# Turning the recurrence's blocks as four 128x128 transposes, gating by channel, and one masked product replaced by a transpose

## The chip, the cores and the metric

One core of one Trainium2 chip runs the whole program once; nothing is shared with other cores. The metric is the time of that one execution on the device in microseconds (us). The engines are named as in the profile: PE is TensorE (matrix products and transposes, into PSUM), PEld its loading of the stationary operand, DVE is VectorE, ACT is ScalarE, POOL is GpSimd, SP is SyncE. Each engine works through its own list of instructions in order and waits on semaphores.

## What is computed

Two transformer layers of another kind follow this one; the change lies in the first, a hybrid layer on 512 tokens of width 1024. One of its two branches is an RWKV-7 recurrence with 8 heads of 64 channels, run forwards and backwards:

```python
def wkv7_scan(r, w, k, v, a, b, reverse):
    def step(S, inp):
        r_t, w_t, k_t, v_t, a_t, b_t = inp
        sa = jnp.einsum('bhij,bhj->bhi', S, a_t)
        S = S * w_t[:, :, None, :] + sa[..., None] * b_t[:, :, None, :] + v_t[..., None] * k_t[:, :, None, :]
        return S, jnp.einsum('bhij,bhj->bhi', S, r_t)
...
    g = jax.nn.sigmoid(xg) @ g_up
...
    y = ((wkv - mean) * lax.rsqrt(var + GN_EPS)).reshape(B, T, RWKV_DIM) * gn_w + gn_b
    y = y + bonus.reshape(B, T, RWKV_DIM).astype(jnp.float32)
    return (y * g).astype(u.dtype)
```

## The kernel before

**Tiles.** The recurrence is worked in 8 chunks of 64 tokens. A tile of it is 128x512: its upper 64 partitions are one head of a pair, its lower 64 the other, and its 512 columns are the 8 chunks of 64. It is stored either by channel (partition = channel, column = token of the chunk) or by token (partition = token within the chunk, column = channel). `turned` (L1020) goes from one to the other: 16 products of 64x64 with the 64x64 identity `ist`, one for each chunk and head, all in place. `each` (L1013) makes the 16 products of 64x64 of two tiles in the same way. On the chip such a product is two matmul instructions, so a group of 16 shows as x32 in the profile.

**Four pairs, two directions.** `recurrence_order` (L724) is the one list from which all engines take their order. For each head pair `pr` (0 to 3) there are preparation steps i = 5 to 28, and in each step direction d = 0 comes first and d = 1 second. Steps 5, 6, 7 turn Aa, Bb and Kt into An, Bn and Kn (`TURNS`). Steps 8 to 12 make the masked products of `MASKS`: MakT, Mrb, Mrk, Dm and Dt, where DVE multiplies the bank by the mask, and for Dt writes a second tile Lt with another mask. Step 13 is R0 = Dt + identity on DVE. Steps 14 to 28 are `PRODS`, which solve a triangular system by repeated squaring: Dt2, D2, R0a, D4 and so on; step 25 is KV, 26 Hc, 27 U1 and 28 W1T. ACT copies out the banks of An, Bn, Kn and the names in `BY_ACT`; DVE those of the others. For pair 0 steps 5 to 7 lie in `front_order`, among the products of the first projection.

**One bank for each direction.** `CHAIN_BANKS = ((4, 4), (5, 5))`: direction 0 has PSUM bank 4, direction 1 bank 5. So `clear(b)` makes PE wait, before each step of a direction, until the step before it has been copied out of the bank.

**What lies between.** After most steps `more()` gives PE one filler, six 128x512 or twelve 128x256 matmuls of the attention and gate projections, into banks 0 to 3. There is none after steps 5, 9, 14, 19 and 24, and after step 12 and step 13 (which has no product) there are two in a row. Beside the preparation of a pair DVE also normalises the pair before it (`rw_norming`, steps 5 to 13), normalises the next pair's keys (`rw_kk`), makes `halfL` = `ring` - `halfH` for each weight tile (ACT makes `halfH` first), and adds up one slice of another product in each step (`m_acc`, from `m_in`, which POOL loads by DMA). `rw_kk` and the transposes of the attention's q and k (the event "turn") share bank 6, with one waiting for the other's copy.

**Gate and turn.** In step 25 of pairs 1 to 3 `rw_gated` makes the gate by token (16 matmuls with `gup`, bank 4), and DVE multiplies y of the pair before by it; in step 27 `rw_turned` turns y by 16 products into bank 5, ACT copies it out as `yH` and DVE makes `yL` = bank - `yH`. The last pair's y is gated and turned in steps 11 to 14 of the attention that follows (`BETWEEN`, L793). `rw_values` turns v into `Vn` once for each pair, through bank 7.

Of the kernel before, what the change touches and what calls it, by code (L numbers as in the profile page):

```python
# [8 lines left out]
F32 = mybir.dt.float32  # L9
# [223 lines left out]
def program(nc, T, out):  # L233
# [175 lines left out]
    for d in range(2):  # L409
# [9 lines left out]
    PRODS = [("Dt2", "Dm", "Dt", None, "Dt"), ("D2", "Dt", "Dm", None, "Dt"), ("R0a", "D2", "R0", "R0", "D2"),  # L419
# [7 lines left out]
    MASKS = [("MakT", "Kt", "Aa", ("US", "LS")), ("Mrb", "Bb", "R", ("UI", "LI")), ("Mrk", "Kt", "R", ("UI", "LI")),  # L427
             ("Dm", "Aa", "Bb", ("DL", "DU")), ("Dt", "Bb", "Aa", ("DU", "DL"))]
# [295 lines left out]
    def recurrence_order():  # L724
# [25 lines left out]
        for pr in range(4):  # L750
# [3 lines left out]
            for i in range(i0, N_PREP):  # L754
                for d in range(2):
                    yield "prep", pr, d, i
                if (i - 4) * 19 // 24 > (i - 5) * 19 // 24:
                    yield from more()
                if pr < 3 and i < i0 + 5:
                    yield "kk", pr + 1, ("squares", "sums", "root", "inverse", "spread")[i - i0]  # L760
                if pr and 5 <= i < 14:
                    yield "norming", pr - 1, i - 5
                if pr and i in (25, 27):
                    yield ("gated", "turned")[(i - 25) // 2], pr - 1
                for _ in range(2 if not pr and i in (16, 20, 24) else 1):
                    yield "ada",
                yield from event(i > 8)
# [20 lines left out]
            for x in early:  # L788
# [4 lines left out]
    BETWEEN = {**{1 + i: ("norming", 3, i) for i in range(9)}, 11: ("gated", 3), 12: ("gated_out", 3), 13: ("turned", 3),  # L793
               14: ("turned_out", 3)}
# [74 lines left out]
    def tensor_program(pe):  # L869
# [189 lines left out]
        def rw_values(pr):  # L1059
            b = ADA_BANK  # L1060
            clear(b)
            pe.wait_ge(*at("us", 8 + pr))
            turned(bank(b), US[:, 8 + pr, :]).then_inc(*up("rw_pe", "v_turned", pr))
            free[b] = [("Vn", pr)]

        def rw_prep(pr, d, i):
            b = CHAIN_BANKS[d][i % 2]
            if 5 <= i < 8:
# [3 lines left out]
                turned(bank(b), piece(d, src)).then_inc(*up(f"rw_pe{d}", "pe", pr, d, name))  # L1072
                free[b] = [("ev", pr, d, name)]
            elif 8 <= i < 13:
# [82 lines left out]
        def rw_gated(pr):  # L1157
            b = CHAIN_BANKS[0][1]
            clear(b)
            for c in range(8):  # L1160
                for h in range(2):
                    i = pe.matmul(bank(b)[HP[h], c * 64:c * 64 + 64], US[:, 13, c * 64:c * 64 + 64],
                                  gup[:, (2 * pr + h) * 64:(2 * pr + h) * 64 + 64], start=True, stop=True)
            i.then_inc(*up("rw_pe", "gate", pr))
            free[b] = [("Y_gated", pr)]

        def rw_turned(pr):
            b = CHAIN_BANKS[1][1]
            clear(b)
            pe.wait_ge(*at("Y_gated", pr))  # L1170
            turned(bank(b), US[:, pr, :]).then_inc(*up("rw_pe", "y_turned", pr))
            free[b] = [("yL", pr)]
# [463 lines left out]
    def scalar_program(ac):  # L1636
# [104 lines left out]

        def rw_values(pr):
            ac.wait_ge(*at("v_turned", pr))
            if pr > 1:
                ac.wait_ge(*at("t3", pr - 2))
            if pr == 0:
                ac.wait_ge(*at("lsplit", FIRST_WOVEN - 1))
            ac.activation(Vn[pr % 2], bank(ADA_BANK), COPY).then_inc(*up("rw_act", "Vn", pr))
# [11 lines left out]
        def rw_prep(pr, d, i):  # L1760
            if 5 <= i < 8:
# [3 lines left out]
                ac.activation(piece(d, name), bank(CHAIN_BANKS[d][i % 2]),  # L1765
                              COPY).then_inc(*up(f"rw_act{d}", "ev", pr, d, name))
# [288 lines left out]
        def tables():  # L2055
# [3 lines left out]
                    "turned": rw_turned, "gemm": rw_gemm, "spill": rw_spill, "ms": a1_ms, "turn": a1_turn,  # L2059
# [34 lines left out]
        def a1_finish(hp):  # L2094
# [30 lines left out]
    def vector_program(ve):  # L2125
# [898 lines left out]
        def tables():  # L3024
            ve.wait_ge(*at("masks"))
            rope_tables("t1")
            for n, g in enumerate([col("gqk", 0)] + [col(f"gab{L}", g) for L in range(2) for g in (0, 2)]):
# [3 lines left out]
                    "loop": rw_loop, "norming": rw_norming, "gated": rw_gated, "turned": rw_turned, "ada": rw_ada, "mods_out": rw_mods_out,  # L3031
# [53 lines left out]
        def a1_finish(hp):  # L3085
# [338 lines left out]
```

## Time and profile before

| | |
|---|---|
| three runs | 2806.80, 2803.65, 2805.99 us (median 2805.99) |
| the profiled execution | 2804.09 us, of which its span is 2802.3 us |
| PE busy | 2696.4 us, 96% of the span |
| DVE busy | 1570.2 us, 56% |
| ACT busy | 926.3 us, 33% |
| the chain that ended last | PE 81%, DMA 8%, DVE 7%, ACT 3% |
| the recurrence (with its front) | about 92 to 610 us |

The chain is followed back from the last instruction, at each step to what released it. A row of the time line is: start in us, duration in us, engine, line, operation, out<-in, shapes, count, and in brackets the idle time before it with what ended it. Lines of one kind are merged, so a row of x64 is two groups of 16 products. A duration is that of the merged row from first start to last end, and since matmuls and ACT instructions overlap their neighbours, the distance from one start to the next start is what a piece costs its engine. A line number of the profile is that of the recording helper (L154 a matmul, L157 a transpose, L160 an ACT instruction, L163 a tensor_tensor), so the names of the tiles tell what it is; `slot` stands for any of the recurrence's scratch tiles.

### The profile page before, as it was taken

Reading aid. Unit: us, or ns where it says so; the run is one execution under the profiler, and the core shown is the slowest. Engines: PE = TensorE matmul, PEld = TensorE weight load, DVE = VectorE, ACT = ScalarE, POOL = GpSimd, SP = SyncE. Lnnn points to the kernel's source line nnn. Section 1 sums busy time; section 2 is a strip of 40 time slices with the busy share of each in tenths; the row PEclk is TensorE's granted clock in tenths of the full one; section 3 lists DMA queues with packets and bytes.
Section 4 is the critical chain, followed back from the end, with each engine's and each line's share of the span. In section 5 each row is a group of like instructions: output and inputs, shape, how many; then the busy total and the mean of one; then the engine's idle time right before and its main releaser. Section 6 shows DMA issues by size and latency. Waiting matters only on the chain.

```text
span 2802.3 us, 46790 instructions
## 1 busy us (share of the span) xinstructions
PE 2696.4 (96%) x20072; PEld 1996.9 (71%) x20072; DVE 1570.2 (56%) x2947; ACT 926.3 (33%) x1559; POOL 138.3 (5%) x237
## 2 busy tenths in 40 slices
PE   8999999999899999989999999999999999999999
PEld 6878777877643333357777778888877777788887
DVE  5767575766443333355685556665466864633443
ACT  6233333236301000033445542223334455332231
POOL 1010100010000000000000000000000000000000
PEclk9999999999999999999999999999999999999999
DMA  4233333264599999963352336664232532232332
GB/s 159 83 111 118 93 103 119 88 216 157 228 389 427 426 425 426 427 236 92 94 115 104 122 109 186 201 192 133 78 106 79 128 113 98 78 103 98 98 97 76
DMA packets 149990, 471.74 MB, mean 168 GB/s; under 512 B 14640, under 2 KB 41888, under 8 KB 137232
## 3 DMA queue, kind: packets, MB, share of 16 engines
q1 hardware_dynamic: 114720, 367.62, 36.6%
q0 software_dynamic: 24976, 82.71, 9.4%
q10 hardware_dynamic: 10080, 18.35, 2.2%
q8 instruction: 160, 2.62, 0.4%
q14 instruction: 54, 0.44, 0.1%
HBM read 451.05 MB, written 21.51 MB: 169 GB/s over the span
## 4 chain that ended last, share of the span: by engine, by line
PE 81%; DMA 8%; DVE 7%; ACT 3%; issue 1%; SPq 0%; ACTq 0%; POOL 0%; DVEq 0%
PE psum L154 78%; DMA wslot<-in_w_up 3%; DMA wslot<-in_w_gate 3%; PE psum L157 3%; DVE halfL L163 1%; DMA m_in<-in_w_ada 1%; DVE slot L163 1%; DVE X L163 1%; ACT halfH L160 1%; DVE vb L163 0%; DVE n_ht L169 0%; DVE gx L163 0%; DVE hL L169 0%; DVE m_acc L169 0%; DMA X<-in_x 0%
## 5 line engine op out<-in xcount | busy, mean ns | idle before, releaser
L163 DVE TENSOR_TENSOR halfL<-ring,halfH 128x1024 fp32r<-128x1024 f32 x302 | 367.9, 1220 | 531.3 <-ACT halfH L160 530.7
L160 ACT ACTIVATE halfH<-ring 128x1024 fp32r<-128x1024 f32 x302 | 317.2, 1053 | 691.7 <-PE psum L154 689.7
L154 PE MATMUL psum<-hH,halfH 128*128 128x512 f32 x1200 | 482.1, 402 | 1.7 <-DVE hL L169 1.7
L154 PE MATMUL psum<-hH,halfL 128*128 128x512 f32 x1200 | 469.1, 391 | 0.0
L154 PE MATMUL psum<-hL,halfH 128*128 128x512 f32 x1200 | 469.0, 391 | 0.0
L154 PEld LDWEIGHTS psum<-hH,halfH 128*128 128x128 f32 x1200 | 225.7, 188 | 74.8 <-issue 24.2
L154 PEld LDWEIGHTS psum<-hH,halfL 128*128 128x128 f32 x1200 | 225.8, 188 | 48.2
L154 PEld LDWEIGHTS psum<-hL,halfH 128*128 128x128 f32 x1200 | 226.0, 188 | 43.3
L154 PE MATMUL psum<-wslot,XT 128*64 128x512 f32 x1024 | 236.3, 604 | 20.0 <-DMA wslot<-in_w_gate 12.8
L154 PE MATMUL psum<-halfH,hH 128*128 128x512 f32 (+2 forms) x576 | 216.7, 376 | 3.7 <-DVE ks L163 1.8
L154 PE MATMUL psum<-halfL,hH 128*128 128x512 f32 (+2 forms) x576 | 207.2, 360 | 0.0
L154 PE MATMUL psum<-halfH,hL 128*128 128x512 f32 (+2 forms) x576 | 207.2, 360 | 0.0
L154 PEld LDWEIGHTS psum<-wslot,XT 128*64 128x64 f32 x1024 | 72.9, 138 | 158.7 <-issue 145.8
L163 DVE TENSOR_TENSOR X<-X,psum 128x512 f32<-128x512 f32 x136 | 88.2, 682 | 120.7 <-PE psum L154 120.7
L154 PEld LDWEIGHTS psum<-slot,slot 64*64 64x64 f32 x4096 | 124.3, 135 | 23.3 <-issue 12.8
L154 PE MATMUL psum<-slot,slot 64*64 64x64 f32 x4096 | 132.4, 219 | 6.2 <-DVE slot L163 2.3
L154 PE MATMUL psum<-halfH,aH 128*128 128x512 f32 x352 | 136.9, 389 | 0.0
L154 PE MATMUL psum<-halfL,aH 128*128 128x512 f32 x352 | 136.9, 389 | 0.0
L154 PE MATMUL psum<-halfH,aL 128*128 128x512 f32 x352 | 136.9, 389 | 0.0
L154 PEld LDWEIGHTS psum<-halfH,hH 128*128 128x128 f32 x576 | 108.6, 188 | 30.4 <-issue 8.6
L169 DVE SCALAR_TENSOR_TENSOR m_acc<-m_in,cact,m_acc 128x512 f32<-128x512 f32 (+1 forms) x126 | 116.3, 923 | 20.6 <-DMA m_in<-in_w_ada 20.0
L154 PEld LDWEIGHTS psum<-halfH,hL 128*128 128x128 f32 x576 | 108.7, 189 | 17.0
(492 smaller groups left out, 4106.3 us busy)
## 6 DMA issues: line engine op xcount, KB each, us to landing
wslot<-in_w_gate SPq DMA_DIRECT2D x32, 2048.0 KB, 25.0
wslot<-in_w_down SPq DMA_DIRECT2D x32, 2048.0 KB, 25.9
ring<-in_w_in SPq DMA_DIRECT2D x120, 512.0 KB, 3.7
wslot<-in_w_up SPq DMA_DIRECT2D x30, 2048.0 KB, 25.9
ring<-in_w_gu SPq DMA_DIRECT2D x88, 512.0 KB, 3.6
m_in<-in_w_ada POOLq DMA_DIRECT2D x96, 256.0 KB, 3.1
m_in<-in_w_ada POOLq DMA_DIRECT2D x48, 512.0 KB, 4.9
ring<-in_w_down SPq DMA_DIRECT2D x44, 512.0 KB, 3.6
```

Source lines behind the costliest of these rows:

```text
L154: return self.e.matmul(*a, **k)
L157: return self.e.transpose(*a, **k)
L160: return self.e.activation(*a, **k)
L163: return self.e.tensor_tensor(*a, **k)
L169: return self.e.scalar_tensor_tensor(*a, **k)
```

## The change

- **Turns.** `turned_by_two` takes the place of `turned` for An, Bn, Kn, v and y: four 128x128 transposes, each over both heads and two chunks. In the result the block of head h and chunk 2n+c stands at partitions of c and columns of h, so it isn't where the tile wants it. `sorted_out` copies the bank out on ACT in four instructions, each 64 partitions by 4x64 columns, two of them crossing from one half of the partitions to the other.
- **Dm.** `MASKS` begins with Dt (step 8); MakT, Mrb and Mrk follow in steps 9 to 11; in step 12 Dm is the turn of the masked Dt, by `turned_by_two` and `sorted_out` on ACT. DVE's mask for Dm is gone, and the first two of `PRODS` wait for Dm.
- **Gate.** y is turned first (step 25, bank 5), while still ungated, and copied by ACT into `US`; then the gate is one product of `gup` and `US` by channel (step 27, bank 4), DVE multiplies, ACT makes `yH` from `US`, and DVE makes `yL` in a step of its own ("low", step 28). In `BETWEEN` the last pair's steps are turned 11, turned_out 12, gated 13, gated_out 14, low 15.
- QT keeps the old `turned`.

```diff
-    PRODS = [("Dt2", "Dm", "Dt", None, "Dt"), ("D2", "Dt", "Dm", None, "Dt"), ("R0a", "D2", "R0", "R0", "D2"),
+    PRODS = [("Dt2", "Dm", "Dt", None, "Dm"), ("D2", "Dt", "Dm", None, "Dm"), ("R0a", "D2", "R0", "R0", "D2"),
...
-    MASKS = [("MakT", "Kt", "Aa", ("US", "LS")), ("Mrb", "Bb", "R", ("UI", "LI")), ("Mrk", "Kt", "R", ("UI", "LI")),
-             ("Dm", "Aa", "Bb", ("DL", "DU")), ("Dt", "Bb", "Aa", ("DU", "DL"))]
+    MASKS = [("Dt", "Bb", "Aa", ("DU", "DL")), ("MakT", "Kt", "Aa", ("US", "LS")), ("Mrb", "Bb", "R", ("UI", "LI")),
+             ("Mrk", "Kt", "R", ("UI", "LI"))]
...
-                if pr and i in (25, 27):
-                    yield ("gated", "turned")[(i - 25) // 2], pr - 1
+                if pr and i in (25, 27, 28):
+                    yield {25: "turned", 27: "gated", 28: "low"}[i], pr - 1
...
+        def turned_by_two(o, x):
+            for n in range(0, 512, 128):
+                i = pe.transpose(o[:, n:n + 128], x[:, n:n + 128], ident)
+            return i
...
+            elif i == 12:
+                clear(b)
+                pe.wait_ge(*at("ev", pr, d, "Dt"))
+                turned_by_two(bank(b), piece(d, "Dt")).then_inc(*up(f"rw_pe{d}", "pe", pr, d, "Dm"))
+                free[b] = [("ev", pr, d, "Dm")]
...
-            for c in range(8):
-                for h in range(2):
-                    i = pe.matmul(bank(b)[HP[h], c * 64:c * 64 + 64], US[:, 13, c * 64:c * 64 + 64],
-                                  gup[:, (2 * pr + h) * 64:(2 * pr + h) * 64 + 64], start=True, stop=True)
-            i.then_inc(*up("rw_pe", "gate", pr))
+            pe.matmul(bank(b), gup[:, pr * 128:pr * 128 + 128], US[:, 13, :], start=True,
+                      stop=True).then_inc(*up("rw_pe", "gate", pr))
...
+        def sorted_out(o, b):
+
+            to, of = o.rearrange("p (n c x) -> p n c x", c=2, x=64), b.rearrange("p (n h x) -> p n h x", h=2, x=64)
+            for c in range(2):
+                for h in range(2):
+                    i = ac.activation(to[HP[h], :, c, :], of[HP[c], :, h, :], COPY)
+            return i
...
-            ve.tensor_tensor(yL[pr], bank(CHAIN_BANKS[1][1]), yH[pr].bitcast(F32), SU).then_inc(*up(R_, "yL", pr))
+            ve.tensor_tensor(yL[pr], US[:, pr, :], yH[pr].bitcast(F32), SU).then_inc(*up(R_, "yL", pr))
```

PE in steps 5 to 7 of pair 1, first as it was (slot_145, _146, _147 are Aa, Bb, Kt of direction 0; _155, _156, _157 those of direction 1), then as it is:

```order
L154 MATMUL psum<-con,slot_145 64x64 x16
L154 MATMUL psum<-con,slot_155 64x64 x16
L154 MATMUL psum<-con,slot_146 64x64 x16
L154 MATMUL psum<-con,slot_156 64x64 x16
...
L154 MATMUL psum<-con,slot_144 128x2 x4
L154 MATMUL psum<-con,slot_147 64x64 x16
L154 MATMUL psum<-con,slot_157 64x64 x16
```

```order
L157 MATMUL psum<-con,slot_145 128x128 x4
L157 MATMUL psum<-con,slot_155 128x128 x4
L157 MATMUL psum<-con,slot_146 128x128 x4
L157 MATMUL psum<-con,slot_156 128x128 x4
...
L154 MATMUL psum<-con,slot_144 128x2 x4
L157 MATMUL psum<-con,slot_147 128x128 x4
L157 MATMUL psum<-con,slot_157 128x128 x4
```

Nothing moves here; each group of 16 becomes one of 4, with the fillers where they were.

DVE in steps 7 to 9 of pair 1, before and after. slot_140/_150 are MakT of the two directions, slot_142/_152 Dt, slot_143/_153 Lt, kk_n and slot_160 belong to the next pair's keys, US to the normalisation of the pair before:

```order
L163 TENSOR_TENSOR halfL_81<-ring_76,halfH_78 128x1024 [waits split_act]
L163 TENSOR_TENSOR US<-US,mean 128x512 [waits rw_dve]
L169 SCALAR_TENSOR_TENSOR m_acc_136<-m_in_134,cact,m_acc_136 128x512 [waits side_dve,m_in0]
L163 TENSOR_TENSOR slot_140<-psum,con 128x512 [waits rw_pe0]
L163 TENSOR_TENSOR slot_150<-psum,con 128x512 [waits rw_pe1]
L166 TENSOR_SCALAR kk_n<-kk_n 128x8 [waits rw_act]
L184 RECIPROCAL kk_n<-kk_n 128x8 [waits rw_dve]
L163 TENSOR_TENSOR US<-US 128x512 [waits rw_dve]
L169 SCALAR_TENSOR_TENSOR m_acc_136<-m_in_135,cact,m_acc_136 128x512 [waits side_dve,m_in1]
L163 TENSOR_TENSOR Mrb_114<-psum,con 128x512 [waits rw_pe0]
```

```order
L163 TENSOR_TENSOR halfL_81<-ring_76,halfH_78 128x1024 [waits split_act]
L163 TENSOR_TENSOR US<-US,mean 128x512 [waits rw_dve]
L169 SCALAR_TENSOR_TENSOR m_acc_136<-m_in_134,cact,m_acc_136 128x512 [waits side_dve,m_in0]
L163 TENSOR_TENSOR slot_142<-psum,con 128x512 [waits rw_pe0]
L163 TENSOR_TENSOR slot_143<-psum,con 128x512
L163 TENSOR_TENSOR slot_152<-psum,con 128x512 [waits rw_pe1]
L163 TENSOR_TENSOR slot_153<-psum,con 128x512
L166 TENSOR_SCALAR kk_n<-kk_n 128x8 [waits rw_act]
L184 RECIPROCAL kk_n<-kk_n 128x8 [waits rw_dve]
L163 TENSOR_TENSOR US<-US 128x512 [waits rw_dve]
L169 SCALAR_TENSOR_TENSOR m_acc_136<-m_in_135,cact,m_acc_136 128x512 [waits side_dve,m_in1]
L163 TENSOR_TENSOR slot_140<-psum,con 128x512 [waits rw_pe0]
```

The four masks of Dt and Lt stand in step 8 instead of two of MakT, and every mask after them one step later.

PE in steps 25 to 28 of pair 1, before and after. slot_141,slot_146 and slot_151,slot_156 are Hc, slot_141,slot_148 and slot_151,slot_158 are W1T; left out are the fillers and U1:

```order
L154 MATMUL psum<-gup,US 64x64 [waits rw_act0]
...
L154 MATMUL psum<-slot_141,slot_146 64x64 [waits rw_dve]
...
L154 MATMUL psum<-slot_151,slot_156 64x64 [waits rw_act1]
...
L154 MATMUL psum<-con,US 64x64 [waits rw_act1]
...
L154 MATMUL psum<-slot_141,slot_148 64x64 [waits rw_act0]
...
L154 MATMUL psum<-slot_151,slot_158 64x64 [waits rw_dve]
```

```order
L157 MATMUL psum<-con,US 128x128 [waits rw_dve,rw_act1]
...
L154 MATMUL psum<-slot_141,slot_146 64x64 [waits rw_act0]
...
L154 MATMUL psum<-slot_151,slot_156 64x64 [waits rw_act]
...
L154 MATMUL psum<-US,gup 128x512 [waits rw_act0]
...
L154 MATMUL psum<-slot_141,slot_148 64x64 [waits rw_dve]
...
L154 MATMUL psum<-slot_151,slot_158 64x64 [waits rw_act1]
```

In step 26 it is now direction 1 that waits, for ACT's copy of the turned y; in step 28 direction 0 waits for DVE's gating, and direction 1 no longer waits for `yL`.

## Rows read from the trace of the kernel before

**Rows 1.** Stretches: us; busy (x count) of PE, PEld, DVE, ACT, POOL; PEclk; DMA.
```profile
272.00:408.00 136.00, 132.06 (x2285) 109.03 (x2280) 89.54 (x182) 42.80 (x68) 12.91 (x24) 1.00 0.34 103
...
620.00:660.00 40.00, 34.50 (x461) 26.03 (x462) 24.52 (x91) 28.99 (x81) 1.63 (x2) 1.00 0.44 163
```

**Rows 2.** Waits of PE, 84 to 620 us: total, times, longest.
```profile
PE psum L154 <- DVE slot L163: 3.3, 6, 1.4
PE psum L154 <- ACT slot L160: 2.4, 6, 0.5
```

**Rows 3.** Time line of PE, pair 2, steps 5 to 7.
```profile
378.25 3.95 PE L154 MATMUL psum<-con,slot 64*64 64x64 f32 x128
382.13 0.50 PE L154 MATMUL psum<-halfH,hH 128*128 128x512 f32 x1
...
383.63 2.96 PE L154 MATMUL psum<-con,slot 128*128 128x2 f32 x72
```

**Rows 4.** Time line of PE: four transposes, a 512-column product (x2), v's turn.
```profile
195.02 0.60 PE L157 MATMUL psum<-con,Zst 128*128 128x128 f32 x4
195.55 1.09 PE L154 MATMUL psum<-colb,slot 64*64 64x1 f32 x32
...
332.57 1.12 PE L154 MATMUL psum<-US,lora 64*128 64x512 f32 x2
...
342.54 1.15 PE L154 MATMUL psum<-con,US 64*64 64x64 f32 x32
343.47 0.33 PE L154 MATMUL psum<-st,W1T 64*64 64x64 f32 x4
```

**Rows 5.** Time line and groups of ACT: copies of 512 and 256 columns, 64 partitions.
```profile
195.65 0.69 ACT L160 ACTIVATE stage<-psum,g 128x512 f32<-128x512 f32 x1 [0.47 <-PE psum L157]
...
288.47 0.38 ACT L160 ACTIVATE Zst<-psum 128x256 f32<-128x256 f32 x1
288.75 0.38 ACT L160 ACTIVATE psum<-psum 128x256 f32<-128x256 f32 x1
...
379.44 0.60 ACT L160 ACTIVATE slot<-psum 128x512 f32<-128x512 f32 x1 [9.33 <-PE psum L154]
...
L160 ACT ACTIVATE US<-US 64x512 f32<-64x512 f32 x1 | 0.6, 633 | 1.2 <-DVE US L169 1.2
```

**Rows 6.** Time line of ACT, DVE and PE, pair 1, steps 7 to 10.
```profile
253.13 1.05 ACT L160 ACTIVATE halfH<-ring 128x1024 fp32r<-128x1024 f32 x1
...
254.21 1.23 DVE L163 TENSOR_TENSOR halfL<-ring,halfH 128x1024 fp32r<-128x1024 f32 x1 [6.29 <-ACT halfH L160]
...
256.62 1.28 DVE L163 TENSOR_TENSOR slot<-psum,con 128x512 f32<-128x512 f32 x2
...
261.60 0.66 PE L157 MATMUL psum<-con,Zst 128*128 128x128 f32 x4 [0.79 <-DVE slot L163]
```

**Rows 7.** Time line of PE: products 14 to 15 begin, pairs 2 and 3.
```profile
408.81 3.36 PE L154 MATMUL psum<-slot,slot 64*64 64x64 f32 x108
...
544.56 3.95 PE L154 MATMUL psum<-slot,slot 64*64 64x64 f32 x128
```

**Rows 8.** Time line of PE, pair 1, steps 25 to 28.
```profile
313.95 1.15 PE L154 MATMUL psum<-gup,US 128*64 128x64 f32 x32
315.90 2.08 PE L154 MATMUL psum<-slot,slot 64*64 64x64 f32 x64 [0.79 <-DVE US L163]
...
323.10 1.15 PE L154 MATMUL psum<-con,US 64*64 64x64 f32 x32
...
325.67 1.15 PE L154 MATMUL psum<-slot,slot 64*64 64x64 f32 x32 [0.49 <-DVE yL L163]
326.75 0.50 PE L154 MATMUL psum<-hH,halfH 128*128 128x512 f32 x1
```

**Rows 9.** Time line of ACT and PE in the front, after step 7 of pair 0.
```profile
110.46 2.06 ACT L160 ACTIVATE U<-psum 128x512 f32<-128x512 f32 x4
...
111.20 0.47 PE L154 MATMUL psum<-halfH,hH 128*128 128x512 f32 x1 [1.28 <-ACT U L160]
```

More of the change, by code:

```diff
@@ L790, in recurrence_order @@
         assert not events and not sums
-    BETWEEN = {**{1 + i: ("norming", 3, i) for i in range(9)}, 11: ("gated", 3), 12: ("gated_out", 3), 13: ("turned", 3),
-               14: ("turned_out", 3)}
+    BETWEEN = {**{1 + i: ("norming", 3, i) for i in range(9)}, 11: ("turned", 3), 12: ("turned_out", 3), 13: ("gated", 3),
+               14: ("gated_out", 3), 15: ("low", 3)}
     def chunk_at(d, s):
@@ L1062, in rw_values @@
             pe.wait_ge(*at("us", 8 + pr))
-            turned(bank(b), US[:, 8 + pr, :]).then_inc(*up("rw_pe", "v_turned", pr))
+            turned_by_two(bank(b), US[:, 8 + pr, :]).then_inc(*up("rw_pe", "v_turned", pr))
             free[b] = [("Vn", pr)]
@@ L1071, in rw_prep @@
                 pe.wait_ge(*at("ev", pr, d, "Aa"))
-                turned(bank(b), piece(d, src)).then_inc(*up(f"rw_pe{d}", "pe", pr, d, name))
+                turned_by_two(bank(b), piece(d, src)).then_inc(*up(f"rw_pe{d}", "pe", pr, d, name))
                 free[b] = [("ev", pr, d, name)]
-            elif 8 <= i < 13:
+            elif i == 12:
[3 more added lines that the diff above has]
+                free[b] = [("ev", pr, d, "Dm")]
+            elif 8 <= i < 12:
                 name, left, right, _ = MASKS[i - 8]
@@ L1169, in rw_turned @@
             clear(b)
-            pe.wait_ge(*at("Y_gated", pr))
-            turned(bank(b), US[:, pr, :]).then_inc(*up("rw_pe", "y_turned", pr))
-            free[b] = [("yL", pr)]
+            pe.wait_ge(*at("Y_sum", pr))
+            turned_by_two(bank(b), US[:, pr, :]).then_inc(*up("rw_pe", "y_turned", pr))
+            free[b] = [("yT", pr)]
         def modulation(L):
@@ L1747, in rw_values @@
                 ac.wait_ge(*at("lsplit", FIRST_WOVEN - 1))
-            ac.activation(Vn[pr % 2], bank(ADA_BANK), COPY).then_inc(*up("rw_act", "Vn", pr))
+            sorted_out(Vn[pr % 2], bank(ADA_BANK)).then_inc(*up("rw_act", "Vn", pr))
         def rw_early(pr, d, x):
@@ L1764, in rw_prep @@
                 ac.wait_ge(*at("pe", pr, d, name))
-                ac.activation(piece(d, name), bank(CHAIN_BANKS[d][i % 2]),
-                              COPY).then_inc(*up(f"rw_act{d}", "ev", pr, d, name))
+                sorted_out(piece(d, name), bank(CHAIN_BANKS[d][i % 2])).then_inc(*up(f"rw_act{d}", "ev", pr, d, name))
+            elif i == 12:
+                ac.wait_ge(*at("pe", pr, d, "Dm"))
+                sorted_out(piece(d, "Dm"), bank(CHAIN_BANKS[d][i % 2])).then_inc(*up(f"rw_act{d}", "ev", pr, d, "Dm"))
             elif i >= 14 and PRODS[i - 14][0] in BY_ACT:
@@ L1779, in rw_turned, with rw_gated @@
             ac.wait_ge(*at("y_turned", pr))
-            ac.activation(yH[pr], bank(CHAIN_BANKS[1][1]), COPY).then_inc(*up("rw_act", "yH", pr))
+            sorted_out(US[:, 4 + pr, :], bank(CHAIN_BANKS[1][1])).then_inc(*up("rw_act", "yT", pr))
+        def rw_gated(pr):
+            ac.wait_ge(*at("Y_gated", pr))
+            ac.activation(yH[pr], US[:, pr, :], COPY).then_inc(*up("rw_act", "yH", pr))
         spilled, turned_last = [0], [None]
```

20 lines of the change are left out of this document (10 added, 10 removed).

## The prediction

> **What bounds the kernel now.** The page first: PE is busy for 96% of the span and 81% of the chain that ended last lies on it. The change lies between 92 and 610 us, so I read the stretches next: from 272 to 408 us PE is busy for 132.06 of 136 us at full clock, DVE for two thirds, ACT for one third [rows 1]. In this stretch every microsecond that PE doesn't need is a microsecond won, unless PE then waits for a copy out of its bank. The waits tell how near that is: from 84 to 620 us PE stood 3.3 us for DVE's tiles and 2.4 us for ACT's [rows 2]. Little is waited now because the fillers just cover the copies. So the question is not what the transposes save, but where the cover ends. For that I walked the time lines of PE, ACT and DVE through each pair.
>
> **Prices.** Four old turns run from 378.25 to 382.13 us: 0.97 us each [rows 3]. Four 128x128 transposes of the same form take 195.02 to 195.55, 0.53 us [rows 4]. So a turn gives PE 0.44 us back. The copy on ACT was 0.60 us. It becomes four pieces of 256 columns; two copies of that size start 0.28 us apart and one lasts 0.38 [rows 5], and 64 partitions by 512 columns take 0.63 us, as much as 128 by 512 [rows 5], so I price by columns: 3 x 0.28 + 0.38 = 1.22 us until the tile is there, 4 x 0.28 = 1.12 us of ACT. No row shows the piece itself; from below it can't be cheaper than those 0.28, from above it costs at most what full copies cost, 2.06 us for four, (2.06 - 0.60) / 3 = 0.49 apart [rows 9]. I take 0.28, since the column count is what the rows of ACT differ by. ACT starts 0.63 us after the first transpose (195.02 to 195.65 [rows 4, 5]); from the end of a copy to PE I take 0.05 us, an estimate from there being no gap in the four groups of [rows 3], whose third needs the copy that ends at 380.04 [rows 5].
> The Trainium skill ("ScalarE: Activation LUTs", What ACT_TABLE_LOAD costs) gives an ACTIVATE without pointers 186 ns + 0.833 ns an element with 93 ns overlap: by it a piece is 0.40 us, 0.31 us apart, and the four take 1.32 us instead of 1.22, which would take 1 to 2 us off my sum.
>
> **Gross.** 24 turns of An, Bn, Kn, 4 of v, 4 of y and 8 of Dm: 40 x 0.44 = 17.6 us. The gate gives nothing: its 16 matmuls last 1.15 us as the profile has them [rows 8], and the nearest single product of 512 columns, the one with `lora`, 1.12 us [rows 4].
>
> **What of it is lost, step by step.**
> *Steps 5 and 6* have no filler between them. From PE's first transpose: copy d0 0.63 to 1.85, PE takes step 6 d0 at 1.90; copy d1 can only start at 1.75 (ACT), ends at 2.97; step 6 d1 at 3.02, filler at 3.55. Before: 3.88 [rows 3]. So four turns give 0.33 us, not 1.76: over four pairs 1.3.
> *Step 7* has fillers on both sides (1.50 us [rows 3]) and keeps its 0.9 a pair. The Bn copies end before it is due, the Kn copies before step 8 is.
> *Pair 0* does this in the front, and there the copies of U stand behind those of Kn on ACT and PE already waits 1.28 us for the first [rows 9]. Two Kn copies of 1.12 in place of 0.5 push U back: PE resumes 0.35 us later than now, so its 1.2 is gone. v gives 0.5, step 10 waits 0.3 for MakT's mask, step 12 gives 0.9: together 0.75.
> *Steps 8 to 11.* Dt and Lt in step 8 put 4 masks of 0.64 (2.5 us) where 2 stood (1.28 [rows 6]), just before step 9, after which there is no filler. In **pair 1** DVE comes late to them whatever PE does: ACT makes `halfH` only behind Kn (253.13, unchanged, since Kn's copy is longer), then halfL at 254.21, then two more, so the masks begin at 256.62 [rows 6], when PE is already 1.2 us ahead. Direction 0 of step 9 waits until 257.9, the keys' product and MakT's masks follow, and the transposes that now stand at 261.60 [rows 6] come at 262.55, 0.95 late. Step 12 gives 0.9 back: at product 14 pair 1 has won nothing. In **pair 2** the `halfH` comes before Kn and DVE is free: the same walk puts product 14 at 406.7 instead of 408.81 [rows 7], 2.1 won. In **pair 3** DVE idles before step 8; the waits left are 0.3 (step 10) and 0.9 (step 11, where it waits 1.1 already), and product 14 comes at 542.6 instead of 544.56 [rows 7], 1.95 won.
> *Step 12* has two fillers behind it and no product in 13, 4 us for two copies that need 0.63 + 2 x 1.12: hidden. If that cover were gone it would cost 1 us a pair.
> *DVE* loses 8 masks, 5 us, none of it on the path by itself.
> *Steps 25 and 26:* now gate to filler is 1.0 + 0.79 of wait + 2.0 = 3.95 us (the next filler after 315.90 is 2.0 later) [rows 8]. Then: turn 0.53, Hc d0 1.0, d1 waits for y's copy until 0.63 + 1.22 + 0.05 = 1.90, ends 2.9: 1.05 won in pairs 1 and 3, 0.85 in pair 2. *Steps 27 and 28:* now 323.10 to 326.75, 3.65 [rows 8]; then the gate 1.05, W1T d0 waits for DVE's product (0.2 + 0.69 + 0.05), then 2.0: 4.0, so 0.35 lost each. Three pairs: 2.95 - 1.05 = 1.9.
> *v in the loops:* 0.93 (342.54 to 343.47) to 0.53 [rows 4], 3 x 0.4 = 1.2; its copy has idle ACT around it.
> *The last pair's y* lies in the attention, where ACT is the busy engine (29 of 40 us [rows 1]): the turn is shorter, but ACT gets 1.2 us more. I put nothing, with 1 us either way.
> What follows (merges, experts) is started by these steps' ends and moves along.
>
> **Sum.** 0.75 + 0 + 2.1 + 1.95 in the preparations, 1.9 for y, 1.2 for v: 7.9, say 8 us of 17.6. Against the profiled execution 2804.09 - 8 = 2796.1; that execution lies 1.9 us under the median of the runs, so 2798.
>
> **Rivals.**
> 1. *The covers hold better.* DVE has 5 us less to do and part of the 3.3 us that PE waits for it [rows 2] goes as well; pair 1 recovers. Gain 12 to 18, time 2788 to 2794. For it: DVE is a third idle. Against: an in-order list fixes when it comes to the masks.
> 2. *The Dt masks cost every pair what they cost pair 1.* Then pairs 2 and 3 lose their 2 us each as well: gain 4, time 2802, within 0.2%. For it: it is enough that `halfH` or an `m_acc` (waiting for its DMA) comes 1 to 2 us later; against: the walks of both pairs had DVE idle ahead of step 8.
> 3. *Slower: the piece is priced by instruction, not by column.* At 0.49 us apart a copy takes 2.07 us. Steps 5 and 6 then take 5.2 us instead of 3.88 (1.7 worse than forecast, four times), steps 7 and 8 wait for the Bn and Kn copies (2 us a pair), Dm's copies outlast their fillers (0.4), y's copy holds Hc (0.85 three times): 19 us, against the 8 won, 2806 + 11 = 2817. It decides from 0.28 + 0.21 x 8 / 19 = 0.37 us a piece. Against it: 0.28 for 256 columns [rows 5].
> 4. *The clock.* In 620 to 660 us a group of four transposes stands every 2 us and the granted clock is 1.00 [rows 1], the 2.4 GHz level. Were it to fall to 1.2 GHz for the 10 us around steps 5 to 8 of each pair, 40 us would be lost: 2838. The Trainium skill ("TensorE: Matmul & The Clock Gate", Part 4: PE-mode transpose) says that transposes don't count as activity for the clock; this trace shows no fall where they are mixed with products.
>
> **Chances.** My walk 0.50 (2794 to 2800), rival 1 0.10, rival 2 and kin 0.30, rival 3 0.08, the clock 0.02. A measurement of this kernel can tell about 0.2% (5.6 us) from no change: faster by more 0.60, within 0.30, slower 0.10. Range: up to the edge of rival 1's half, 2789, and over rival 2 with some waits more, 2808; rivals 3 and 4 are left out.
>
> **What would show it.** Steps 5 and 6 of pair 2 at 3.5 us from first transpose to filler (3.88 now), with PE waiting for ACT's tiles: in all about 10 us of such waits where 2.4 are. ACT's pieces at 0.38 us, 0.28 apart. In pair 1 PE waits for DVE before step 9, about 1.5 us, and product 14 starts no earlier against step 5 than now (31.1 us); in pairs 2 and 3 about 2 us earlier. Step 25 to filler 2.9 us, step 27 to filler 4.0. PE's busy time down by 15 to 18 us. Wrong would be the whole if ACT's piece were over 0.37 us apart or the clock showed under 1.00 in these stretches; wrong in size if DVE were late in pair 2 or 3, or early in pair 1.

## The result, and the profile after

The changed kernel takes 2818.39 us, median of five runs (2811.32 to 2823.75), against 2805.99 before: ratio 1.0045, 95% interval 1.0033 to 1.0057, slower by 12.6 us. Forecast were 2798 us and a range up to 2808. The profiled execution took 2819.83 us with a span of 2818.0, and the granted clock over the whole was 0.988 where it had been 0.994.

PE's busy time fell by only 8 us (2696.4 to 2688.5), and PE waits more. First its waits from 84 to 670 us in the trace after (total, times, longest), against [rows 2], whose two sums are the same when the trace before is read to 670 us:

```profile
PE psum L157 <- ACT slot L160: 9.0, 8, 1.8
PE psum L154 <- DVE slot L163: 6.7, 7, 2.3
PE psum L154 <- ACT slot L160: 5.6, 10, 1.6
PE psum L154 <- ACT U L160: 4.2, 1, 4.2
```

The first row is the transposes themselves (L157), waiting for ACT to empty the bank. It had no counterpart before. Some stretches of the trace after, with the columns of [rows 1]; the last but two is the granted clock, which was 1.00 in all of them before:

```profile
112.00:142.00 30.00, 27.66 (x335) 23.05 (x336) 20.09 (x32) 8.39 (x16) 1.61 (x3) 0.89 0.27 80
...
240.00:272.00 32.00, 26.73 (x320) 21.55 (x320) 17.50 (x34) 13.92 (x31) 2.15 (x4) 0.89 0.26 75
...
378.00:408.00 30.00, 27.59 (x327) 21.88 (x323) 17.78 (x40) 12.64 (x28) 1.75 (x4) 0.94 0.24 74
```

**Where the time goes** can be read by laying the same step of PE side by side in both time lines. The lag (start after minus start before):

| step of PE | before | after | lag |
|---|---|---|---|
| pair 0, step 5 | 98.25 | 98.47 | 0.2 |
| pair 0, first masked product (step 8) | 123.58 | 127.85 | 4.3 |
| pair 0, product 14 | 143.58 | 146.94 | 3.4 |
| pair 1, step 5 | 244.25 | 247.88 | 3.6 |
| pair 1, step 8 | 254.11 | 258.36 | 4.3 |
| pair 1, product 14 | 275.36 | 283.22 | 7.9 |
| pair 1, product 19 | 292.00 | 304.43 | 12.4 |
| pair 2, step 5 | 378.25 | 391.50 | 13.3 |
| pair 2, product 14 | 408.81 | 421.79 | 13.0 |
| pair 3, step 5 | 514.57 | 528.61 | 14.0 |
| pair 3, product 14 | 544.56 | 558.33 | 13.8 |
| attention, first scores | 614.17 | 628.17 | 14.0 |

So the front and pair 1 lose nearly all of it, 12.4 us. Pairs 2 and 3 break even up to product 14, and what follows product 19 in pair 1 and product 14 in pair 2 loses about 1 us each. At the large product stages the lag is 12.6 (the run that starts at 1663.57 us before, 1676.18 after). By the end of the span it is 15.7: the profiled execution after loses 3 us more behind 2030 us, in work that the change doesn't touch. Its granted clock there is 0.82 in 2032 to 2040 us and 0.79 in 2112 to 2120 and 2448 to 2456 us, where the trace before has 1.00 in the same work. That part I don't count to the change; the medians differ by 12.4 us.

*The front.* Time line of PE after, from step 5 of pair 0:

```profile
98.47 1.03 PE L157 MATMUL psum<-con,slot 128*128 128x128 f32 x8
101.28 0.66 PE L157 MATMUL psum<-con,slot 128*128 128x128 f32 x4 [1.77 <-ACT slot L160]
102.85 0.66 PE L157 MATMUL psum<-con,slot 128*128 128x128 f32 x4 [0.91 <-ACT slot L160]
...
108.81 1.03 PE L157 MATMUL psum<-con,slot 128*128 128x128 f32 x8
114.04 0.77 PE L154 MATMUL psum<-halfH,hH 128*128 128x512 f32 x1 [4.19 <-ACT U L160]
114.60 0.63 PE L154 MATMUL psum<-halfL,hH 128*128 128x512 f32 x1
```

Two turns take 1.03 us, as forecast, and then PE stands 1.77, 0.91 and, after step 7, 4.19 us; the last was 1.28 in [rows 9]. The products behind it last 0.63 us and start 0.43 apart, where 0.39 and 0.23 is normal: ten of them, 2.1 us more, until the clock is back at 118.8 us.

*Pair 2, steps 5 to 7*, the place of [rows 3]: PE first, then ACT.

```profile
391.50 1.03 PE L157 MATMUL psum<-con,slot 128*128 128x128 f32 x8
393.73 0.66 PE L157 MATMUL psum<-con,slot 128*128 128x128 f32 x4 [1.20 <-ACT slot L160]
395.30 1.11 PE L157 MATMUL psum<-con,slot 128*128 128x128 f32 x4 [0.91 <-ACT slot L160]
396.06 0.78 PE L154 MATMUL psum<-halfH,hH 128*128 128x512 f32 x1
396.64 0.63 PE L154 MATMUL psum<-halfL,hH 128*128 128x512 f32 x1
```
```profile
392.13 3.12 ACT L160 ACTIVATE slot<-psum 64x256 f32<-64x256 f32 x8 [8.68 <-PE psum L157]
395.27 3.12 ACT L160 ACTIVATE Bn<-psum 64x256 f32<-64x256 f32 x8
398.41 1.06 ACT L160 ACTIVATE halfH<-ring 128x1024 fp32r<-128x1024 f32 x1
```

Eight pieces in 3.12 us: 0.39 us apart, each 378 ns long, so they don't overlap. A copy takes 1.57 us; the forecast was 1.22. From the first transpose to the filler it is 4.56 us (3.88 before, 3.55 forecast), and the filler itself runs slow.

*Pair 1* shows what stands behind the pieces on ACT's list. ACT, DVE and PE after, steps 7 to 9, the place of [rows 6]:

```profile
256.63 3.12 ACT L160 ACTIVATE Kn<-psum 64x256 f32<-64x256 f32 x8 [1.86 <-PE psum L157]
259.77 1.06 ACT L160 ACTIVATE halfH<-ring 128x1024 fp32r<-128x1024 f32 x1
```
```profile
260.86 1.23 DVE L163 TENSOR_TENSOR halfL<-ring,halfH 128x1024 fp32r<-128x1024 f32 x1 [9.21 <-ACT halfH L160]
...
263.27 2.48 DVE L163 TENSOR_TENSOR slot<-psum,con 128x512 f32<-128x512 f32 x4
```
```profile
264.61 3.17 PE L154 MATMUL psum<-slot,slot 64*64 64x64 f32 x64 [2.06 <-DVE slot L163]
267.70 1.69 PE L154 MATMUL psum<-con,kk_n 128*64 128x128 f32 x16
```

`halfH` comes 6.64 us later than before (253.13): 3.6 of it is the lag with which pair 1 begins, 1.3 the later start of Kn's pieces behind step 5, and 1.7 their length. DVE waits 9.21 us for it with the masks queued behind, PE waits 2.06 us for the masks, and then works at the lower clock: 3.17 us for what takes 2.08. The same chain comes a second time, behind Dm's copies:

```profile
281.62 3.12 ACT L160 ACTIVATE slot<-psum 64x256 f32<-64x256 f32 x8 [0.40 <-ACT stage L160]
284.76 1.06 ACT L160 ACTIVATE halfH<-ring 128x1024 fp32r<-128x1024 f32 x1
```
```profile
285.85 1.23 DVE L163 TENSOR_TENSOR halfL<-ring,halfH 128x1024 fp32r<-128x1024 f32 x1 [6.93 <-ACT halfH L160]
...
295.75 0.75 DVE L169 SCALAR_TENSOR_TENSOR m_acc<-m_in,cact,m_acc 128x512 f32<-128x512 f32 x1 [2.76 <-DMA m_in<-in_w_ada]
```
```profile
287.49 2.08 PE L154 MATMUL psum<-slot,slot 64*64 64x64 f32 x64 [1.55 <-ACT slot L160]
...
297.16 2.08 PE L154 MATMUL psum<-slot,slot 64*64 64x64 f32 x64 [2.33 <-DVE slot L163]
```

DVE is held from 278.9 to 285.85 us, so it gives the modulation's `m_in` buffers back late, their next loads land late, and the sum that PE wants for product 17 stands behind an `m_acc` that waits for its DMA. (This last link, from the buffers to the loads, is read from the order of the rows; no run tries it by itself.) That costs 4.6 us between product 14 and 19 (21.21 us against 16.64).

### The profile page after: what moved, and what is told of

Read it like the earlier page. It is cut to its first block, busy times and chain, and to the rows that moved or that the text cites. A ratio compares the mean times of both kernels' runs of the same rounds, so it can differ in the third digit from the quotient of the medians.

```text
span 2818.0 us, 44435 instructions
## 1 busy us (share of the span) xinstructions
PE 2688.5 (95%) x18832; PEld 1985.4 (70%) x18832; DVE 1565.6 (56%) x2939; ACT 970.4 (34%) x1691; POOL 137.6 (5%) x237
## 4 chain that ended last, share of the span: by engine, by line
PE 80%; DMA 8%; DVE 6%; ACT 4%; issue 2%; ACTq 0%; SPq 0%; POOL 0%; DVEq 0%
PE psum L154 76%; PE psum L157 4%; DMA wslot<-in_w_gate 3%; DMA wslot<-in_w_up 3%; DVE halfL L163 1%; ACT slot L160 1%; ACT halfH L160 1%; DVE X L163 1%; DMA m_in<-in_w_ada 1%; DVE slot L163 0%; DVE vb L163 0%; ACT Kn L160 0%; DVE gx L163 0%; DMA X<-in_x 0%; DVE b_ss L175 0%
## 5 line engine op out<-in xcount | busy, mean ns | idle before, releaser
L154 PEld LDWEIGHTS psum<-slot,slot 64*64 64x64 f32 x3840 | 117.9, 135 | 33.1 <-issue 12.3
L154 PE MATMUL psum<-slot,slot 64*64 64x64 f32 x3840 | 126.6, 221 | 14.1 <-DVE slot L163 6.2
```

Source lines behind the costliest of these rows:

```text
L154: return self.e.matmul(*a, **k)
```

## Experiments

Three theories stood after this reading. **A**: the copy in four pieces (1.57 us against 0.60) holds PE at steps 5 to 7 and everything behind it on ACT. **B**: Dt first, and Dm as a turn, cost it in pair 1. **C**: the granted clock falls around the transposes; whether through PE's idle time or through the transposes themselves was to be told apart. In the edits shown, `+` is the kernel of the run, and lines are shortened. Each kernel ran against the kernel before on the same chip; ratios are to that.

### One part undone: the turns of An, Bn and Kn (e1)

```
-   turned_by_two(bank(b), piece(d, src))       # PE, steps 5 to 7
+   turned(bank(b), piece(d, src))
-   sorted_out(piece(d, name), bank(...))       # ACT
+   ac.activation(piece(d, name), bank(...), COPY)
```

> The changed kernel, but An, Bn and Kn (steps 5 to 7) turned by 64x64 matmuls and copied in one piece as before; v, y, the gate, Dt first and Dm as a turn of Dt stay. Theory A (the copy in four pieces holds PE, and whatever stands behind it on ACT, in steps 5 to 7): the profile of the change puts 4.0 us of the lag in the front (PE waits 4.19 us for U) and some 2 us more in steps 5 to 7 of each later pair, so 8 to 12 of the 12.4 us come back: 2806 to 2810 us, and PE's 4.19 us wait for U falls back to 1.3. Theory B (Dt first, with its two masks a direction, and Dm's turn behind it cost it, 9 us in pair 1 between the first mask product and QT): the time stays at 2813 or above, and pair 1's waits of 2.06 us (first masks) and 2.33 us (product 17) stay.

2806.3 us, ratio 0.9997 (0.9989 to 1.0006). Between 1.0045 and this lie 13.5 us: undoing the 24 turns two by two takes the whole loss away, as A has it, with about 4 us of uncertainty either way. Its waits show U back at what it was:

```profile
PE psum L154 <- ACT U L160: 1.3, 1, 1.3
```

B isn't nothing, though: PE's waits of 1.55 us (product 15) and 1.86 us (product 17) of pair 1 stand in this trace too, and from product 14 to 19 it needs 20.3 us against 16.6. So the rest of the change wins about as much elsewhere as Dm's turn loses there.

### The copy shared between two engines (e2)

```
-   sorted_out(piece(d, name), bank(...))            # ACT: four pieces
+   sorted_out(piece(d, name), bank(...), (0,))      # ACT: two
+   for h in range(2):                               # DVE: the other two
+       ve.tensor_copy(to[HP[h], :, 1, :], of[HP[1], :, h, :])
```

> The changed kernel, but of the four 64x256 pieces of each copy of An, Bn and Kn two are on ACT and two on DVE, side by side; all else stays. Theory A: a copy takes 0.78 us in place of 1.56, shorter than the 0.97 us of an old turn, so steps 5 to 7 hold PE no longer and the gross gain is kept: 2796 to 2804 us, faster than before or equal. Theory B: 2810 or above, since the masks are as they were. Theory C (TensorE's granted clock falls because of the 128x128 transposes themselves, whatever they wait for): the granted clock in 92 to 142 us stays near 0.93 and the matmuls behind the turns still take 0.63 us in place of 0.39, some 5 us in all: 2803 to 2809.

2811.32 us, ratio 1.0013 (1.0004 to 1.0022): better than the change by 9 us, but not the 2796 to 2804 that I expected of A. The copy is shorter only where DVE is free. Its pieces take 427 ns, and in the front it was not free; its group, and PE there:

```profile
L181 DVE COPY slot<-psum 64x256 f32<-64x256 f32 x16 | 6.8, 427 | 1.4 <-PE psum L157 1.1
```
```profile
102.51 1.98 PE L157 MATMUL psum<-con,slot 128*128 128x128 f32 x8 [2.58 <-DVE slot L181]
104.15 0.77 PE L154 MATMUL psum<-hH,halfH 128*128 128x512 f32 x1
```

DVE did its part only behind `halfL`, which waited for ACT's `halfH`; PE stood 2.58 us and the clock fell, with the wait moved from ACT to DVE. In 92 to 142 us, where I had named a clock near 0.93 as the mark of the transposes as cause, it is 0.97: 0.72 in 102 to 108 us, around that wait, and 1.00 from 112 us on.

### The pieces alone, no transpose (e3, e12)

```
-   ac.activation(piece(d, name), bank(...), COPY)                    # kernel before
+   for h in HP:
+       for x in (0, 256):
+           ac.activation(piece(d, name)[h, x:x + 256], bank(...)[h, x:x + 256], COPY)
```

> The kernel before, but each copy of An, Bn and Kn by ACT is in four pieces of 64x256 (contiguous halves, the same result); no transpose, no other part of the change. Theory A: the pieces stand 0.39 us apart, a copy takes 1.56 us in place of 0.60, longer than the 0.97 us between two turns; 1.2 to 1.8 us in steps 5 and 6 of each pair, 2 us at U in the front, and what ACT does behind it (half H, masks on DVE) 1 to 2 us late in pair 1: 2812 to 2817 us. Theory B, or theory C with the transposes as the cause of the fall of the clock: at most 2809, granted clock 0.994 as before.

2813.06 us, ratio 1.0022 (1.0013 to 1.0031): the kernel before with nothing but its copies cut in four loses 6 us, half of what the change loses. It is the second proof of A, here without the rest. ACT, and PE in the front behind its wait for U:

```profile
99.64 2.64 ACT L160 ACTIVATE slot<-psum 64x256 f32<-64x256 f32 x8
```
```profile
113.73 0.47 PE L154 MATMUL psum<-halfH,hH 128*128 128x512 f32 x1 [2.57 <-ACT U L160]
...
115.20 0.63 PE L154 MATMUL psum<-halfH,hH 128*128 128x512 f32 x1
```

The lower clock (0.63 us a product) comes here too, 1.5 us after PE has resumed, and this kernel has no transpose there. But its pieces stand 0.33 us apart, not 0.39. They differ from the change's in two things: 256 columns in a row, and each on its own partitions. e12 has the first as in the change (every other chunk of 64) and the second as in e3:

> As e3 (the kernel before, copies of An, Bn and Kn in four pieces), but each piece takes every other chunk of 64 columns, read and written so, on its own partitions. e3's pieces stood 0.33 us apart and the change's 0.39. If the chunks of 64 make the difference: 0.39; if the move to other partitions does: 0.33.

```profile
100.09 2.64 ACT L160 ACTIVATE slot<-psum 64x256 f32<-64x256 f32 x8
```

Again 0.33. So the chunks cost nothing; what is left as the difference are the pieces that write to the other 64 partitions (and with it the order of the pieces over the partitions, which wasn't tried by itself). e12 took 2811.75 us in its one run.

### PSUM laid out for the reader (e8)

```
-   pe.transpose(o[:, n:n + 128], x[:, n:n + 128], ident)
+   pe.transpose(to[:, n], x[:, n * 128:n * 128 + 128], ident)   # to: "p (h n x) -> p n h x"
```

> The changed kernel, but the turns write PSUM so that each of the four pieces is read as 256 consecutive words of a partition, and only written in chunks of 64; same instructions, same order. The pieces stood 0.39 us apart in the change and 0.33 in e3, where both sides were consecutive and no piece changed its partitions. If the strided read is the difference: 0.33 apart, a copy takes 1.34 us in place of 1.57, and 1 to 3 us less than the change: 2815 to 2817. If the move to other partitions or the strided write is: 0.39 as before and 2817 to 2820.

2819.26 us, ratio 1.0049 (1.0036 to 1.0062), the change's time. Its pieces are as far apart:

```profile
99.63 3.11 ACT L160 ACTIVATE slot<-psum 64x256 f32<-64x256 f32 x8
```

With e12 this closes the layout as a cause.

### PE's waits filled with work (e4, e9)

```
+   if (i, d) == (6, 0):
+       unused(16)
+   if (i, d) == (6, 1):
+       unused(10)
...
+   for m in range(n):                       # unused(n)
+       pe.matmul(bank(ADA_BANK)[h, cc], SL[0]["Aa"][h, cc], ist[h, :], start=True, stop=True)
```

> The changed kernel with 64x64 matmuls that nobody reads put where PE waits in its trace: 16 ahead of step 6 of the first direction (gap 1.20 us), 10 ahead of the second (gap 0.91), 56 behind step 7 of pair 0 (gap 4.19), 30 ahead of step 9 of pair 1 (gap 2.06). The waits themselves stay as they are. If PE's idle time is what lets the granted clock fall behind the turns (slow rows of 0.63 us for 0.39, and 3.17 for 2.08: 2.2 us in the front, 1.4 and 1.7 in pair 1, 1.7 in pair 2, 7 us in all), the clock stays at 1.00 there and the time falls to 2810 to 2813. If the transposes are the cause, or the slow rows lie in time that waits hide, 2817 to 2821.

2810.91 us, ratio 1.0013 (1.0004 to 1.0021): 9 us under the change (4 either way), for matmuls that nobody reads. The front, with 56 of them (112 records) behind step 7:

```profile
106.86 1.03 PE L157 MATMUL psum<-con,slot 128*128 128x128 f32 x8
107.82 3.48 PE L154 MATMUL psum<-con,slot 64*64 64x64 f32 x112
112.08 0.47 PE L154 MATMUL psum<-halfH,hH 128*128 128x512 f32 x1 [0.78 <-ACT U L160]
```

U comes as late behind step 7 as in the change (5.2 us); the product behind it takes 0.47 us and not 0.77, and the granted clock is 1.00 in 112 to 120 us where the change has 0.58, and in 262 to 270 and 394 to 402 us, where it has 0.79 and 0.79. So C holds, with PE's idle time as the trigger at these places. Does it have to be products? e9 fills the same places with 128x128 transposes:

> As e4, but the stretches in which PE waits are filled with 128x128 transposes that nobody reads (7, 4, 26 and 14 of them, about the same time as the 64x64 matmuls of e4). If the granted clock falls because PE stands idle: the clock stays at 1.00 behind the turns as in e4, ratio 1.0005 to 1.0020. If PE's transposes don't hold the clock up: it falls as in the change (slow rows of 0.63 us behind the turns, 0.58 granted in 112 to 120 us), ratio 1.0035 to 1.0055.

2811.04 us, ratio 1.0026 (1.0015 to 1.0037), 5 us under the change (again 4 to 5 either way). The ratio lies between what I had named for the two theories; the records decide:

```profile
107.18 3.87 PE L157 MATMUL psum<-con,slot 128*128 128x128 f32 x34
112.41 0.47 PE L154 MATMUL psum<-halfH,hH 128*128 128x512 f32 x1 [1.36 <-ACT U L160]
```

34 transposes in a row, 1.36 us of wait, and the product behind runs at full speed; the clock is 1.00 in the same three stretches. Here transposes held it up as products did. The clock costs 5 to 9 us of the loss by these two kernels; by the slow rows of the change I had counted 7.

Not every wait has that effect. In the change, full speed follows on waits of 1.77 and 0.91 us in steps 5 and 6 of pair 0, on 1.20 and 0.92 us in pair 3, and on 2.33 us at product 17 of pair 1, while 1.20 and 0.91 us were enough in pairs 1 and 2. In e4 the clock falls at another place, 0.79 in 280 to 288 us, where nothing was filled. What tells these cases apart the runs don't show.

### The order of the masks, and Dm's turn (e5, e6)

e5 is the kernel before with Dt first, e6 the change with Dm by its own product and the old order.

```
-   MASKS = [("MakT", ...), ("Mrb", ...), ("Mrk", ...), ("Dm", ...), ("Dt", ...)]
+   MASKS = [("Dt", ...), ("MakT", ...), ("Mrb", ...), ("Mrk", ...), ("Dm", ...)]      # e5
```

> The kernel before, but Dt first among the five masked products (Dt, MakT, Mrb, Mrk, Dm), Dm still by its own product; no transpose in blocks of 128 is added. Theory B (the order alone costs it, since the first masks on DVE are four in place of two): PE's wait behind the first masks grows by 1.2 us and stays in pair 1, where e1 had nothing to spare: 2808 to 2811. Theory B2 (the order is nearly free; what costs in e1, 3.4 us between product 14 and product 19 of pair 1, is Dm's copy in pieces on ACT, which holds the stage copies and half H, and by half H the modulation's loads): at most 1 us, 2806 to 2808, and no wait above 1 us at products 15 and 17 of pair 1.

2806.37 us, ratio 1.0000 (0.9989 to 1.0011). The order alone costs nothing that can be measured. In its trace pair 1 needs 16.4 us from product 14 to 19, as before, and doesn't wait at products 15 and 17; so what e1 loses there (20.3 us) comes from Dm's turn and its copies, not from the order.

> The changed kernel, but Dm by its own masked product and the masks in the old order; An, Bn, Kn, v and y are turned two by two and sorted out as in the change. Theory A: steps 5 to 7 keep their cost, and of the masks' part 4.2 us of PE time is given up (four times 1.05) while some 5 to 7 us of pair 1's waits go: 2812 to 2817. Theory B (order and Dm's turn are the whole loss): 2803 to 2808.

2819.3 us, ratio 1.0039 (1.0025 to 1.0053). The median is a little above my span for A, the ratio (some 2816 us) inside it, and both are far from B. Of its waits, those for ACT in the turns and for U are the change's; that for DVE is 1.8 us shorter, and PE's other wait for ACT's tiles is 2.4 us as in the kernel before, where the change has 5.6:

```profile
PE psum L157 <- ACT slot L160: 9.0, 8, 1.8
PE psum L154 <- DVE slot L163: 4.9, 7, 1.7
PE psum L154 <- ACT slot L160: 2.4, 6, 0.5
PE psum L154 <- ACT U L160: 4.2, 1, 4.2
```

So Dm as a turn in all pairs is worth nothing that can be measured (1.0045 with it, 1.0039 without). That it saves in pairs 0, 2 and 3 what it gives away behind product 14 of pair 1 is how I read it; e10 below bears it out.

### The front alone (e11)

```
-   turned_by_two(bank(b), piece(d, src))
+   (turned_by_two if pr else turned)(bank(b), piece(d, src))    # and ACT's copy likewise
```

> The changed kernel, but An, Bn and Kn of pair 0 alone (in the front) turned and copied as before. The change's trace puts 4.0 us of the lag between step 5 and the first masks of pair 0 (PE waits 4.19 us for U in place of 1.28, and 11 matmuls behind it take 0.63 us in place of 0.39): the ratio falls by 0.0014 from the change's 1.0045, to 1.0025 to 1.0037. If pairs 1 to 3 give the time away whatever the front does, it stays above 1.004.

2809.83 us, ratio 1.0016 (1.0002 to 1.0031): 8 us back for six of the 24 turns, where I had read 4 off the trace; the interval is wide enough for both. Its own trace has 24.5 us from step 5 of pair 0 to the first masked product (98.17 to 122.68), where the change takes 29.4: 4.9 us back in the front itself. Another 3 come at 616 to 624 us, where the change's clock is 0.79 and that of e11 is 1.00. By the traces the front costs 4 to 5 us and pair 1 about 9.

### What is worth keeping (e7, e10)

> Only v, y and the gate of the change: An, Bn, Kn turned and copied as before, the masks as before. From the change's trace: y 0.67 us less a pair between product 25 and the bonus for pairs 0 to 2, v 0.5 less three times and once in the front, pair 3's y in the attention stage 0.7 more (2.3 us of wait for the sorted y, 1.6 for yL before): 3 us less than before, 2802 to 2805. If the covers are worse than those rows say, 2806 to 2808.

e7 (only v, y and the gate) took 2804.45 us, ratio 0.9997 (0.9988 to 1.0006): with the measurement's width, between nothing and the 3 us I had worked out. The loop of pair 2 gives some of it back: PE waits 2.4 us for `SA` there, 1.5 before; its cause I didn't follow.

e10 takes all that paid: v, y and the gate, and Dm as a turn except in pair 1.

```
+   elif i == 12 and pr == 1:
+       each(bank(b), piece(d, "Aa"), piece(d, "Bb"))     # Dm by its own product
    elif i == 12:
        turned_by_two(bank(b), piece(d, "Dt"))
```

> A version meant to be the best of the parts: v, y and the gate of the change, Dt first, Dm as a turn of Dt in pairs 0, 2 and 3 and by its own masked product in pair 1, An, Bn and Kn turned as before. Against e1, pair 1 gets back the 3.4 us between products 14 and 19: 2801 to 2804, ratio 0.9985 to 0.9992. If PE's time that Dm's turn saves is waited away in the other pairs too: as e7, 0.9992 to 1.0002.

2802.49 us, ratio 0.9989 (0.9979 to 0.9999), 3 us under the kernel before (0.3 to 6) and the fastest of all. Pair 1 has its 16.4 us from product 14 to 19 back:

```profile
273.40 3.95 PE L154 MATMUL psum<-slot,slot 64*64 64x64 f32 x128
...
289.83 2.39 PE L154 MATMUL psum<-slot,slot 64*64 64x64 f32 x72
```

## Why the prediction was wrong, step by step

- **What bounds the kernel** (PE, with covers that just hold [rows 1, 2]) was right, and so was the question where the cover ends. The PE price was right too: 0.53 us a turn, 1.03 for two.
- **The copy: this term failed.** I took 0.28 us between pieces from two copies of 128 partitions [rows 5], with 0.28 and 0.49 as bounds and 0.37 as the point from which the change loses. It measured 0.39. The row of 64 partitions by which I argued that columns set the price reads and writes `US`, so it isn't a copy out of a bank at all. The row that I chose as nearest was near in columns, but its copies stayed on their partitions; e3 and e12 have 0.33 for such pieces of 64 partitions, and 0.39 comes with the change's own, two of which cross over. Both lie above the value that I took. By the formula of the Trainium skill ("ScalarE: Activation LUTs", What ACT_TABLE_LOAD costs), which it gives for tiles of 128 partitions, a piece of 256 columns is estimated at 0.40 us. The 378 ns here come near to that, but where the page has 93 ns of overlap between neighbours, e3 shows 0.04 us and the change none.
- **Steps 5 and 6**: 3.55 forecast, 4.56 measured. With 1.57 us a copy the walk as I wrote it gives 4.35 (copy d1 ends at 0.63 + 3.14, then 0.05, and 0.53 for step 6 d1); the other 0.2 is the slow clock, which makes those last transposes take 0.76. The walk was right; its number was not.
- **Pair 0**: forecast +0.75, measured -3.1 (lag 0.2 to 3.4). I had U 0.35 us later; it was 2.84 us later (113.30, before 110.46). Of this 1.0 is that step 7 itself begins later, behind the waits of steps 5 and 6, and 1.7 that from Kn's first piece to U it is now 3.14 us in place of 1.43. ACT's `halfH` stands ahead of Kn's copies in both kernels and is not the cause. The clock's 2.1 us stands on top.
- **Pair 1**: I forecast nothing won, on the ground that ACT makes `halfH` at 253.13 whatever Kn's copy does. That sentence failed first: `halfH` stands behind Kn's copies on ACT, and these took 3.12 us, 1.4 times what I had priced and twice what they took before, and began later. The second loss, behind Dm's copies, was missing altogether. I wrote of step 12 "4 us for two copies that need 0.63 + 2 x 1.12: hidden", which looks at PE's need alone and not at `halfH` and the stage copies behind those copies on ACT. Of the 8.8 us that pair 1 loses from step 5 to product 19, 4.6 are this.
- **Pairs 2 and 3**: 2.1 and 1.95 forecast, 0.3 and 0.3 measured from step 5 to product 14 (30.56 to 30.29, 29.99 to 29.72). What Dm's turn gives there steps 5 and 6 take.
- **y and v**: turn to filler 2.9 us forecast, 3.31 measured; gate to filler 4.0 forecast, 4.1 measured (rows below, of pair 1). With v I had summed 3.1 us; e7 measures 0.8 with some 2.5 either way. (For the gate as it was I wrote 1.0 + 0.79 + 2.0, which is 3.79; the 3.95 that I used is right by [rows 8], where the gate lasts 1.15.) The last pair's y, which I put at nothing with 1 us either way, loses 1.6: the lag is 14.0 at the first scores and 15.6 at its first product (`yH`, 659.88 before, 675.44 after). By 1663 us all of that and more has come back.

```profile
326.29 0.60 PE L157 MATMUL psum<-con,US 128*128 128x128 f32 x4
...
328.52 1.15 PE L154 MATMUL psum<-slot,slot 64*64 64x64 f32 x32 [0.56 <-ACT US L160]
329.60 0.50 PE L154 MATMUL psum<-hH,halfH 128*128 128x512 f32 x1
...
334.69 1.02 PE L154 MATMUL psum<-US,gup 128*128 128x512 f32 x2
336.76 2.08 PE L154 MATMUL psum<-slot,slot 64*64 64x64 f32 x64 [1.06 <-DVE US L163]
338.78 0.50 PE L154 MATMUL psum<-hH,halfH 128*128 128x512 f32 x1
```

- **The rivals.** Rival 3 named the mechanism (the piece dearer than its columns) and gave 2817; I gave it 0.08. It assumed 0.49 apart; at 0.39 its own line gives 19 x 0.11 / 0.21 - 8 = 2 us lost. The other 10 it didn't have: the clock (5 to 9), and the chain over `halfH` and `m_in`. Rival 4, the clock, was right that it falls around steps 5 to 8, and wrong in size (7 us, not 40: PE works for 3 to 5 us at the lower level, not 10, and in pair 3 not at all) and in cause: it asked whether transposes hold the clock up, while here it fell behind waits of PE and stayed up when they were filled. My evidence against it, a clock of 1.00 in 620 to 660 us, came from a stretch whose longest wait of PE is 1.64 us; the change made one of 4.19. The Trainium skill's rule that I cited beside it ("TensorE: Matmul & The Clock Gate", Part 4: PE-mode transpose), that transposes don't count as activity for the clock, isn't borne out by e9, where the clock stayed at 1.00 through 34 fp32 transposes.
- **The chances** had the two rivals that came true together at 0.10, as if they were independent of the walk. They weren't: the longer copy makes the waits, and waits let the clock fall.

## What to carry to other kernels

When one instruction on a helper engine becomes four, price it by a row of the same shape and the same move between partitions, or take the upper bound: here 0.11 us a piece turned a forecast gain into a loss. And follow that engine's list past the consumer in question: what stands behind the longer copies (here a weight conversion, through it DVE, through DVE a load) may wait for longer than PE does. Where PE is the bound, a wait can cost more than its length, since the work behind it may run at a lower clock (2.1 us on top of 4.19 in the front).

## What the runs showed of the hardware that I had not expected

- ACT's copies from PSUM of 64 partitions by 256 columns: 0.33 us apart on their own partitions (372 ns each, read in a row or in every other chunk of 64), 0.39 apart in the change, where two of four go to the other partitions (378 ns each, no overlap). DVE's take 427 ns.
- In the front of the change the granted clock is 0.99 in 110 to 112 us and 0.50 (the 1.2 GHz level) from 112 to 118 us, so it fell while PE stood for 4.19 us. For the first 4.7 us after the wait products of 512 columns start 0.43 us apart, 0.23 before and after. Without transposes it fell behind a wait of 2.57 us (e3), and not behind 0.78 (e4) or 1.36 us (e9) with work ahead of them.
- Matmuls that nobody reads, put into PE's waits, made the changed kernel 9 us faster; transposes in their place kept the clock at 1.00 as well.
